# Conditioning products of a two-layer diffusion block: weighed and added over k on VectorE, summed over partitions on TensorE

## What is computed

```python
for i in range(DEPTH):                      # 2 layers
    mx = (silu(c)     @ w_mod[i] + b_mod[i])    # latent condition,  9 x 1024 outputs
    mc = (silu(c_ctx) @ w_mod[i] + b_mod[i])    # context condition, 9 x 1024 outputs
    x   = swiglu_half(x,   mx, 0, ...)
    ctx = swiglu_half(ctx, mc, 0, ...)
    ... mixer, residual ...
    x   = swiglu_half(x,   mx, 2, ...)

def swiglu_half(h, m, k, g_pre, g_post, wg, wu, wd):
    u = modulate(h, g_pre, m[3 * k], m[3 * k + 1])
    y = (silu(u @ wg) * (u @ wu)) @ wd          # 1024 -> 2816 -> 1024
    return gated_residual(h, y, g_post, m[3 * k + 2], 0.5)
```

## Time and profile before

| | |
|---|---|
| median of 3 runs | 2271.11 us (2270.88 to 2272.94) |
| profiled execution, first to last instruction | 2271.0 us; the profile gives no other time of its own for it |
| busy: PE, PEld, DVE, ACT, POOL | 94%, 77%, 47%, 37%, 10% |
| mean DMA rate | 128 GB/s |

### The profile page before, as it was taken

The page is one execution under the profiler, slowest core; times in us unless marked ns, Lnnn a source line. Parts: engine busy times, 40 slices in busy tenths (PEclk is TensorE's granted clock), DMA queues, the critical chain, the costliest instruction groups (busy, mean ns, idle before and its releaser), DMA issues. The chain is left out here.

```text
span 2271.0 us, 29238 instructions
## 1 busy us (share of the span) xinstructions
PE 2143.7 (94%) x12073; PEld 1754.0 (77%) x12073; DVE 1062.9 (47%) x1687; ACT 847.0 (37%) x1452; POOL 233.1 (10%) x220
## 2 busy tenths in 40 slices
PE   6999999998889989899999989999998988899998
PEld 4777777867556768677777788888787776788998
DVE  4332332459778552633332253333225678755554
ACT  3222222335355343422222233222224545654443
POOL 0000000133212300100000010000002442400000
PEclk9999999999999989899999989999998999989999
DMA  7545544222233212345545522332432233333553
GB/s 281 186 158 179 182 153 146 76 77 75 93 93 112 71 59 93 118 161 185 175 161 174 178 73 75 107 97 93 158 102 59 75 112 113 130 130 123 180 185 126
DMA packets 282834, 291.08 MB, mean 128 GB/s; under 512 B 8318, under 2 KB 275534, under 8 KB 282702
## 3 DMA queue, kind: packets, MB, share of 16 engines
q1 hardware_dynamic: 281671, 286.95, 38.6%
q10 hardware_dynamic: 1031, 2.28, 0.3%
HBM read 288.02 MB, written 1.18 MB: 127 GB/s over the span
## 5 line engine op out<-in xcount | busy, mean ns | idle before, releaser
L93 DVE TENSOR_TENSOR split<-raw,split 128x1024 fp32r<-128x1024 f32 (+1 forms) x308 | 369.7, 1200 | 873.5 <-ACT split L85 866.3
L85 ACT ACTIVATE split<-raw 128x1024 fp32r<-128x1024 f32 (+1 forms) x292 | 302.3, 1035 | 891.4 <-PE bank L146 882.3
L144 PE MATMUL bank<-uh,split 128*128 128x512 f32 (+1 forms) x1344 | 493.0, 367 | 1.1 <-DVE split L93 1.1
L145 PE MATMUL bank<-ul,split 128*128 128x512 f32 (+1 forms) x1344 | 488.6, 364 | 0.0
L146 PE MATMUL bank<-uh,split 128*128 128x512 f32 (+1 forms) x1344 | 487.4, 363 | 0.0
L144 PEld LDWEIGHTS bank<-uh,split 128*128 128x128 f32 x1344 | 253.6, 189 | 57.5 <-issue 18.4
L146 PEld LDWEIGHTS bank<-uh,split 128*128 128x128 f32 x1344 | 253.8, 189 | 40.3
L144 PE MATMUL bank<-hh,split 128*128 128x256 f32 (+1 forms) x836 | 283.1, 339 | 0.9 <-DVE split L93 0.9
L145 PEld LDWEIGHTS bank<-ul,split 128*128 128x128 f32 x1344 | 253.7, 189 | 38.1
L145 PE MATMUL bank<-hl,split 128*128 128x256 f32 (+1 forms) x836 | 279.2, 334 | 0.0
L146 PE MATMUL bank<-hh,split 128*128 128x256 f32 (+1 forms) x836 | 278.6, 333 | 0.0
(11 more groups left out here) (226 smaller groups left out, 2595.6 us busy)
## 6 DMA issues: line engine op xcount, KB each, us to landing
raw_mod<-in_w_mod SPq DMA_DIRECT2D x64, 1024.0 KB, 7.5
raw<-in_ffn_w_gate SPq DMA_DIRECT2D x44, 1024.0 KB, 5.2
raw<-in_ffn_w_up SPq DMA_DIRECT2D x44, 1024.0 KB, 5.2
raw<-in_w_in SPq DMA_DIRECT2D x40, 1024.0 KB, 5.1
raw<-in_ffn_w_down SPq DMA_DIRECT2D x32, 1024.0 KB, 4.8
raw<-in_w_out SPq DMA_DIRECT2D x16, 1024.0 KB, 4.7
raw<-in_ffn_w_down SPq DMA_DIRECT2D x16, 768.0 KB, 4.2
decay<-cum_rows SPq DMA_DIRECT2D x48, 256.0 KB, 3.7
```

Source lines behind the costliest of these rows:

```text
L85: ins = K.nc.scalar.activation(K.wh[:, half, 0:kn, :], K.raw[:, slot, 0:kn, half * P:half * P + P], ACT.Copy)
L93: ins = K.nc.vector.tensor_tensor(K.wl[:, half, 0:kn, :], K.raw[:, slot, 0:kn, half * P:half * P + P], r32(K.wh[:, half, 0:kn, :]), ALU.su ...
L144: K.nc.tensor.matmul(bank[:, 0:tn], K.wh[:, half, k, :], h, start=first and k == 0, stop=False)
L145: K.nc.tensor.matmul(bank[:, 0:tn], K.wh[:, half, k, :], l, start=False, stop=False)
```

## The change

Each w_mod element is now multiplied by the two conditions on DVE and the eight k blocks are added up there, in `mod_acc`; PE only sums over the 128 partitions.

- Weights come in *chunks* of 2 k blocks by 512 columns (512 KB) into three slots. A *set* is 4 chunks: 512 columns, 8 k blocks. 4 sets replace 8 panels: 11 sets in a loop, then 3, 5 and (layer 1) 2 sets in down products, 32 together.
- `mod_weigh_dve`: for each of a chunk's k blocks and for each condition one DVE instruction on 128x512: `tensor_scalar` for k = 0 (L205 of the changed kernel), else `scalar_tensor_tensor`, multiply by the condition's column and add to the running sum (L208). 16 per set, 512 in all. Two running sums, one for each condition, alternate, so that each instruction waits for the one before the last.
- `mod_sum_pe`: up to two sets at once, one matmul of 512 columns for each set and condition in a tile of its own, the stationary operand being a column of ones in `unit`. In the loops it stands behind k block 1 of half 0 of trips 2, 4, 6, 8 and 10, and the eleventh set's stands behind half n=0 of the down product; down sets are summed after n = 7, 15 and the last half with a chunk. That makes 6+2, 6+3 and 1 sums, 18 in all.
- In a trip a chunk is weighed behind each low part (before half 2's, behind it, behind half 3's, and between `product(i, 0)` and `hidden_lo(2i)`); in the down product behind the low part of every half n < `mods`.
- Rows, turn and bias (L230, L238, L249) have 512 columns for every group: four turning matmuls, also where a group of a down product had two. They stand one half later.
- SP loads chunks between panels; it waits for DVE's count `mod_step` in place of `mod_mm`. The opening's constants have three more small memsets on POOL, the late parameters are put in `mod_rows`.

```diff
+def load_mod(K, sp, w_mod, q, chunk):
+    k0, c0 = chunk % CHUNKS_PER_SET * CHUNK_K, P * (q + chunk // CHUNKS_PER_SET * MOD_TILES)
+    src = w_mod[k0 * P:(k0 + CHUNK_K) * P, bass.ds(c0, MOD_TILES * P)].rearrange("(k p) n -> p k n", p=P)
+    sp.wait_ge(K.mod_step.sem, K.mod_step.at(CHUNK_STEPS * (chunk - MOD_SLOTS + 1)))
+    sp.dma_start(K.raw_mod[:, chunk % MOD_SLOTS], src).then_inc(K.mod_full[chunk % MOD_SLOTS].inc(16), 16)
+
+def mod_weigh_dve(K, dve, chunk, first, sums):
+    n, part = (chunk - first) // CHUNKS_PER_SET, chunk % CHUNKS_PER_SET
+    full = K.mod_full[chunk % MOD_SLOTS]
+    dve.wait_ge(full.sem, full.landed(chunk // MOD_SLOTS + 1))
+    if part == 0:
+        dve.wait_ge(K.mod_mm.sem, K.mod_mm.at(sums + n // 2))
+    for kk in range(CHUNK_K):
+        k = part * CHUNK_K + kk
+        for s in range(2):
+            total, w = K.mod_acc[:, n % 2, s, :], K.raw_mod[:, chunk % MOD_SLOTS, kk, :]
+            c = K.cond[:, COL - 2 + COL * k + s:COL - 1 + COL * k + s]
+            if k == 0:
+                ins = K.nc.vector.tensor_scalar(total, w, c, None, ALU.mult)
+            else:
+                dve.wait_ge(K.mod_step.sem, K.mod_step.own(1))
+                ins = K.nc.vector.scalar_tensor_tensor(total, w, c, total, ALU.mult, ALU.add)
+            ins.then_inc(K.mod_step.inc(), 1)
+
+def mod_sum_pe(K, pe, n, count, first, group):
+    if group and n == 0:
+        pe.wait_ge(K.mod_row.sem, K.mod_row.at(group))
+    sets = min(2, count - n)
+    pe.wait_ge(K.mod_step.sem, K.mod_step.at(CHUNK_STEPS * (first + CHUNKS_PER_SET * (n + sets))))
+    for i in range(sets):
+        for s in range(2):
+            tile, row = COL * (2 * i + s), 2 * (n + i) + s
+            ins = K.nc.tensor.matmul(K.bank[4][tile:tile + COL, :], K.unit[:, COL - 1 - row:2 * COL - 1 - row], K.mod_acc[:, i, s, :],
+                                     start=n == 0, stop=True, skip_group_check=True)
+    ins.then_inc(K.mod_mm.inc(), 1)
...
@@ OutProduct.pe, behind half n
-                if half and n < self.mods:
-                    full = K.mod_full[h // 2 % 2]
-                    pe.wait_ge(full.sem, full.landed(h // 4 + 1))
-                    mod_mm(K, pe, K.raw_mod[:, h // 2 % 2], h // 2, self.mod_group, self.mod_h // 2)
-                if n == 0 and self.mod_group:
-                    mod_turn_pe(K, pe, self.mod_h // 2, 0)
+                if n == 0 and self.loop_sets % 2:
+                    mod_sum_pe(K, pe, self.loop_sets - 1, self.loop_sets, 0, 0)
+                if n == 1 and self.mod_group:
+                    mod_set_turn_pe(K, pe, 0)
+                if n < self.mods and (n % 8 == 7 or n == self.mods - 1):
+                    mod_sum_pe(K, pe, n // 8 * 2, self.mod_sets, self.mod_h, self.mod_group)
...
@@ OutProduct.dve, behind the low part of half n
-            if n == 0 and self.mod_group:
-                mod_rows_dve(K, dve, self.mod_h // 2 - 1, self.mod_h // 2, 0)
-            if n == 1:
+            if n == 1 and self.mod_group:
+                mod_set_rows_dve(K, dve, self.loop_sums, 0)
+            if n < self.mods:
+                mod_weigh_dve(K, dve, self.mod_h + n, self.mod_h, self.loop_sums)
+            if n == 2:
...
@@ feed_forward, TensorE, trip i
-                    if mods_loop and half % 2:
-                        panel = 2 * i + half // 2
-                        pe.wait_ge(K.mod_full[panel % 2].sem, K.mod_full[panel % 2].landed(panel // 2 + 1))
-                        mod_mm(K, pe, K.raw_mod[:, panel % 2], panel, 0, 0)
+                                     True, True, 4 * i + half, None,
+                                     sums_after if mods_loop and half == 0 and i >= 2 and i % 2 == 0 else None)
...
@@ feed_forward, VectorE, trip i
+                weigh(0)
                 weight_lo(K, dve, 1, 0, 8, 4 * i + 2)
+                weigh(1)
                 weight_lo(K, dve, 1, 1, 8, 4 * i + 3)
+                weigh(2)
...
                 product(i, 0)
+                weigh(3)
                 hidden_lo(2 * i)
                 product(i, 1)
```

More of the change, by code:

```diff
@@ new lines, in mod_set_rows_dve, with mod_set_turn_pe @@
+def mod_set_rows_dve(K, dve, sums, group):
+    dve.wait_ge(K.mod_mm.sem, K.mod_mm.at(sums))
+    dve.wait_ge(K.mod_fold.sem, K.mod_fold.at(group))
+    K.nc.vector.tensor_copy(K.rows[:, :], K.bank[4][:, :]).then_inc(K.mod_row.inc(), 1)
+def mod_set_turn_pe(K, pe, group):
+    pe.wait_ge(K.mod_row.sem, K.mod_row.at(group + 1))
+    pe.wait_ge(K.mod_evac.sem, K.mod_evac.at(group))
+    for t in range(MOD_TILES):
+        ins = K.nc.tensor.matmul(K.bank[7][:, t * COL:t * COL + COL], K.rows[:, t * P:t * P + P], K.fold[:, :], start=True, stop=True)
+    ins.then_inc(K.mod_fold.inc(), 1)
@@ new lines, in mod_set_out_dve @@
+def mod_set_out_dve(K, dve, layer, q, sets, group):
+    dve.wait_ge(K.mod_fold.sem, K.mod_fold.at(group + 1))
+    turned = K.bank[7][:, 0:MOD_TILES * COL].rearrange("p (t j s) -> p t j s", t=MOD_TILES, s=2)[:, :, 0:sets, :]
+    out = K.mod[:, layer, q:q + MOD_TILES * sets, :].rearrange("p (j t) s -> p t j s", t=MOD_TILES)
+    bias = K.par[:, layer, 0, q:q + MOD_TILES * sets].rearrange("p (j t) -> p t j", t=MOD_TILES)
+    for t in range(MOD_TILES):
+        ins = K.nc.vector.tensor_tensor(out[:, t], turned[:, t], bias[:, t].unsqueeze(2).to_broadcast([P, sets, 2]), ALU.add)
+    ins.then_inc(K.mod_evac.inc(), 1)
@@ L219, in mod_turn_pe, with mod_out_dve @@
     ins.then_inc(K.mod_fold.inc(), 1)
-def mod_out_dve(K, dve, layer, q, panels, group, bank=7):
+def mod_out_dve(K, dve, layer, q, panels, group, bank):
     dve.wait_ge(K.mod_fold.sem, K.mod_fold.at(group + 1))
@@ L451, in sp @@
         for p in range(self.n_panels):
[L452 to L453 removed]
+            for c in (2 * p + 1, 2 * p + 2):
+                if (2 if self.mod_h else MOD_SLOTS) <= c < self.mods:
+                    load_mod(K, sp, K.w_mod[self.mod_layer], self.mod_q - self.mod_h, self.mod_h + c)
             if p + 2 < self.n_panels:
@@ L710, in feed_forward @@
             sil = up_mem.enter_context(nc.sbuf_tensor("sil" + tag, [P, 2, TOK], F32))
-            late = LateParams(K, up_mem) if (layer, which) == (0, 0) else None
+            late = LateParams(K) if (layer, which) == (0, 0) else None
         y = mem.enter_context(nc.sbuf_tensor("y" + tag, [P, 8, TOK], F32))
@@ L837, in trip, with weigh @@
             def trip(i, first, last):
+                def weigh(part):
+                    if mods_loop:
+                        mod_weigh_dve(K, dve, CHUNKS_PER_SET * i + part, 0, 0)
                 if not first:
@@ L2091, in hybrid_block @@
         K.raw_full = [signal(f"raw_full{n}") for n in range(2)]
-        K.mod_full = [signal(f"mod_full{n}") for n in range(2)]
+        K.mod_full = [signal(f"mod_full{n}") for n in range(MOD_SLOTS)]
         K.stage_full = [signal(f"stage_full{n}") for n in range(8)]
```

61 lines of the change are left out of this document (37 added, 24 removed).

## The result

Four runs of the changed kernel took 2210.59 to 2216.67 us, median 2213.35; four of the kernel before on the same chip 2270.88 to 2272.94, median 2271.69. The ratio is 0.9745, 95% interval 0.9733 to 0.9757: 2.5% less. Two later sets of five gave medians of 2213.7 and 2215.86, ratios 0.9749 [0.9735, 0.9762] and 0.9750 [0.9737, 0.9764].

What follows compares the result with a forecast made beforehand. PE was taken as the bound: -81.0 us for panels, +22.7 for sums, +1.3 turns, +1.0 waits and +0.1 first trip give -55.9 from 2271.0, so 2215 us. Range 2210 to 2221 (chance 0.80), reaching from 2209 to 2226.

Steps and rivals of the forecast that it cites:

- What bounds: First feed-forward's loop: PE is the bound, 24.29 us a trip with two panels, 21.76 without; two panels cost 2.53 us.
- A sum at 1.26 us: On PE, 18 sums at 1.26 us each, tiles side by side, as much as a panel: 22.7 us added.
- Turns, +1.3: Three groups of down products go from two to four turning matmuls, 0.44 us more each: +1.3 us.
- DVE's price: Weighing on DVE: 0.66 us from start to start, 0.80 as upper bound; `tensor_scalar` 0.5; 17.7 us of DVE a trip.
- The wait before half n=2: Two down products behind conditioning loops: DVE waits for the eleventh set's sum, PE then 0.45 us; +1.0 us (0 to 3).
- First trip and opening: First trip's early chunk on DVE costs 0 to 0.4 us, taken as 0.1; the opening's small memsets on POOL cost nothing.
- The sum: Whole kernel: -55.9 us against the profiled execution's 2271.0, giving 2215 us, 2.5% less.
- A: Loop trips and down product starts: DVE or its order costs PE a few us more, +13 us, 2228; chance 0.13.
- B: Loop trips and down halves with chunks: DVE becomes the bound, slower beyond 1.05 us per instruction; chance 0.03.
- C: Sums on PE: their tiles don't work side by side, +46 us, 2261; chance 0.04 together with D and other mixed ends.
- D: Feed-forward panels weren't on the path that sets the end; no size given; chance 0.04 with C and other mixed ends.
- signs of being wrong: PE waiting at every half for the low part, DVE waiting for `mod_full`, or a gap around a sum over 2 us.

Runs made afterwards that it cites:

- the half panel: Kernel before, with only k blocks 0 to 3 of every feed-forward conditioning panel multiplied: 2238.73 and 2241.73 us, ratio 0.9864.
- both experiments on the sums: Changed kernel with one sum for every set (2231.77 and 2231.72 us), and with all matmuls of a sum in one tile (2251.43, 2258.14 and 2252.2 us).
- the other buffer: Changed kernel with a down product's first set, behind a conditioning loop, in the running-sum buffer no sum still reads: medians 2216.87 and 2214.9 us.
- Measured at 1.00: Changed kernel with one more DVE `tensor_tensor` of 128x256 into scrap ahead of each weighing instruction: 2253.15 and 2252.04 us, ratio 0.9917.

## Why the prediction was right, point by point

- **What bounds.** Right: trips at 21.8 us without and 23.0 with a sum; two panels had cost a trip 2.53 us, and the half panel shows that such time is paid in full.
- **A sum at 1.26 us.** 1.20 by the timeline, 1.23 by the trips; 18 of them 22 us, 22.7 forecast. That the tiles run side by side is confirmed by both experiments on the sums.
- **Turns, +1.3.** Right by the timeline: all five turns after take 0.97 or 0.98 us with eight records, three of those before took 0.53 with four.
- **DVE's price.** 0.66 us from start to start was right to the hundredth (2.73 us for four, so (2.73 - 0.75)/3 = 0.66). For the disputed `tensor_scalar` I had taken 0.5 between 0.3 and 0.75; it is 0.40 (two in 0.88, one in 0.48). The two-operand form in PSUM was the wrong neighbour, the small one in SBUF the right one, and the Trainium skill's rule (VectorE: DVE Perf Modes, "The perf-mode tier table": f32 `tensor_scalar` in SBUF at twice the rate) is borne out: from 128 to 512 columns the duration of `tensor_scalar` grows by 0.66 ns a column (228 to 480), that of the form with two tensors by 1.18 (292 to 747), 1.8 times as much. Together with the part that doesn't grow with the columns that makes 0.40 against 0.66 us from start to start. A trip's DVE time was forecast at 17.7 us and is 17.3.
- **The wait before half n=2.** 0.45 us forecast, 0.45 measured. The mechanism is shown by the other buffer, without which the wait goes. That the size fits so exactly is luck. With `tensor_scalar` at 0.40 in place of 0.50, the first chunk was 0.2 us shorter, and the low part ended 13.3 us behind the start of half n=0, 13.5 forecast. But PE, too, was ready earlier, at 12.9 in place of 13.05, mostly because a turn takes 0.80 us to the next matmul and not 0.90. For a price by the skill's rule the prediction had worked out next to no stall. The price came near the rule's, and the stall was there all the same, since PE came earlier too.
- **First trip and opening.** First matmul of the loop at 40.46 us, 40.61 before, and the first silu 14.9 us behind it in both; nothing lost.
- **The sum.** Span against span -56.1 us, -55.9 forecast; median against median -58.3, and -58.0 and -56.0 in the two later sets. The first two are 2.4 and 2.1 us more than forecast, of which no run shows the place. The profiled execution was the slowest of its four, 3.3 us above their median, that of before about 1.1 above its own; that is the difference between 56.1 and 58.3. In the stages that changed, the windows give -56.4.
- **The rivals.** A: what there was of it is the 0.9 us of the two waits. B: not there at 0.66, as forecast. Its break-even stood at 1.05 us for an instruction, with 7.5 us of other DVE work in a trip, where durations are counted that overlap by 0.1 us each; the experiments reckoned with 7.0. Measured at 1.00 the kernel is at 2252.6 us. From there 0.05 us more would be 0.8 us a trip, 18 us in 22 trips, so the other 19 us would be lost near 1.05: an estimate, no run was made there. C: refuted. Its price was 39 us and not 46, since four of the 18 sums use two tiles and not four. D: refuted by the half panel. Of the signs of being wrong none came: no wait of PE at every half, no wait of DVE for a chunk, 1.20 us around a sum. One part of the account was incomplete: it called the start of the down products the one place where DVE's work doesn't fit, and DVE stood at three more sums.

## What to carry to other kernels

Before moving work to an idle engine, don't ask for its busy share but for its order: what stands behind each moved piece, when that is needed, and how much time lies between. Here 3 us of slack at each low part made 318 us of DVE work free but for 0.9 us, and that loss came where DVE had to wait for PE in between. With column tiles, a sum cost its waves (two of 0.43 us) and about 0.35 us on the ways in and out, whether two or four tiles were in use, so fill the tiles, and join the small products. And a prefetch depth that is enough in the steady state may not be enough behind a burst on the queue that issues it.

## What I had not expected of the hardware

The second mixer's unchanged work took 313.0 us in one profiled execution and 317.3 in another, with granted clocks of 0.95 and 0.94. The timed runs of the changed kernel lie about 6 us apart in each of its three sets, those of the kernel before 2 to 4. Why they lie further apart is not shown.

A wait of PE in dense work can cost more than its length, but need not. Behind one of 1.35 us the clock read 0.93 over 25 us, which cost another 1.6 us; behind an equal one, before the same half of the second down product, it stayed at 1.00. Behind the wait of 1.86 us in the kernel with two slots it read 0.54 over 3.75 us. Which of the two happens can't be told from the length of the wait.
